# Low-rank products ahead of the grouped heads, and their chain spread over earlier steps

## The reference

```python
p_rwkv, p_pool, p_att, p_gate = jnp.split(hn @ w_in, split_at, axis=-1)
p_rwkv = p + mu_prev * (p_prev - p) + mu_next * (p_next - p)      # token shift
r, k, v, wd, ad, gd = jnp.split(p_rwkv, offs, axis=-1)
w_raw = w0 + einsum('bsel,elc->bsec', tanh(wd), w2)               # two directions e
decay = exp(-exp(-softplus(-w_raw) - 0.5))
a = sigmoid(a0 + einsum('bsel,elc->bsec', ad, a2))
kk = k * k_k / max(norm(k * k_k), 1e-12)                          # per head
k_dir = k * (1 + (a - 1) * k_a)
# a recurrence over 256 tokens, both directions, with r, decay, k_dir, v, kk, a
y_b = pool_w @ (windowed means of p_pool (2, 4, 8, 16 tokens) - p_pool)
y_c = softmax(q @ k.T) @ v                                        # 8 heads, 2 key heads
x = x + (sum over branches of gate * (branch @ w_branch)) @ w_out
x = x + expert_choice_ffn(rms_norm(x))                            # 16 experts
```

## Time and profile before

| | |
|---|---|
| Median of 3 runs | 1749.14 us (1746.7 to 1750.22) |
| Profiled execution | 1747.45 us |
| Its span | 1745.7 us |
| TensorE, VectorE, ScalarE busy | 1559.4, 841.5, 376.7 us |
| Mean DMA rate | 221 GB/s |

### The profile page before, as it was taken

One profiled execution on the slowest core, in us unless ns is written; L12 is line 12 of the kernel. 1 busy time (PEld: TensorE's weight loads), 2 busy tenths in 40 slices (PEclk: granted clock), 3 DMA queues, 4 the chain that ended last, 5 costly groups with the idle time before them and its releaser, 6 DMA issues.

```text
span 1745.7 us, 26458 instructions
## 1 busy us (share of the span) xinstructions
PE 1559.4 (89%) x10938; PEld 1089.6 (62%) x10938; DVE 841.5 (48%) x1699; ACT 376.7 (22%) x952; POOL 2.1 (0%) x6
## 2 busy tenths in 40 slices
PE   9999999999999999999999999999999656656665
PEld 6877878884488786888647878999853112112111
DVE  6676567665577765665646577564531000000001
ACT  4362131110225422311102571111211000000001
POOL 0000000000000000000000000000000000000000
PEclk9999999999999999999999999999999968878868
DMA  9324335344542242453543322121888999999997
GB/s 392 130 74 163 127 119 212 148 190 169 201 173 97 84 183 72 186 192 145 193 175 145 118 99 92 57 75 52 356 366 345 427 425 423 425 424 425 425 420 327
DMA packets 49474, 386.37 MB, mean 221 GB/s; under 512 B 5584, under 2 KB 6096, under 8 KB 9808
## 3 DMA queue, kind: packets, MB, share of 16 engines
q1 hardware_dynamic: 47376, 375.15, 54.0%
q10 hardware_dynamic: 1984, 9.57, 1.4%
HBM read 383.65 MB, written 1.05 MB: 220 GB/s over the span
## 4 chain that ended last, share of the span: by engine, by line
PE 72%; DMA 21%; DVE 3%; ACT 2%; issue 1%; SPq 0%; DVEq 0%; ACTq 0%
PE ps L217 52%; DMA arena<-in_stream 19%; PE ps L2357 3%; PE ps L1096 2%; DMA const<-in_stream 2%; PE ps L1585 2%; PE ps L221 1%; PE ps L1195 1%; PE ps L745 1%; PE ps L1228 1%; PE ps L1254 1%; PE ps L1686 0%; PE ps L2618 0%; PE ps L646 0%; PE ps L2561 0%
## 5 line engine op out<-in xcount | busy, mean ns | idle before, releaser
L217 PE MATMUL ps<-arena 128*128 128x256 f32 (+4 forms) x2364 | 528.9, 484 | 90.7 <-DMA arena<-in_stream 80.8
L217 PEld LDWEIGHTS ps<-arena 128*128 128x128 f32 (+1 forms) x2364 | 308.5, 172 | 266.9 <-DMA arena<-in_stream 128.4
L217 PE MATMUL ps<-ring,arena 128*128 128x256 f32 (+5 forms) x1172 | 323.3, 508 | 37.1 <-DMA ring<-in_stream 31.4
L217 PEld LDWEIGHTS ps<-ring,arena 128*128 128x128 f32 (+1 forms) x1172 | 178.3, 175 | 158.9 <-issue 78.4
L217 PE MATMUL ps<-arena,ring 128*128 128x256 f32 (+1 forms) x1140 | 233.9, 352 | 0.0
L217 PEld LDWEIGHTS ps<-arena,ring 128*128 128x128 f32 x1140 | 190.0, 190 | 28.5 <-issue 9.6
L3038 DVE TENSOR_TENSOR arena<-arena,ps 128x512 f32<-128x512 f32 x8 | 5.5, 687 | 307.6 <-PE ps L2816 307.6
L2816 PE MATMUL ps<-arena 128*32 128x512 f32 x218 | 137.6, 758 | 0.0
L1143 ACT ACTIVATE arena<-arena,small 128x256 f32<-128x256 f32 x112 | 55.7, 498 | 67.0 <-DVE small L1130 50.6
L217 PE MATMUL ps<-arena,spare 128*128 128x128 f32 x510 | 65.5, 278 | 0.0
L217 PEld LDWEIGHTS ps<-arena,spare 128*128 128x128 f32 x510 | 60.4, 192 | 0.7
(11 more groups left out here) (476 smaller groups left out, 2014.1 us busy)
## 6 DMA issues: line engine op xcount, KB each, us to landing
ring<-in_stream SPq DMA_DIRECT2D x131, 1024.0 KB, 4.9
arena<-in_stream SPq DMA_DIRECT2D x112, 1024.0 KB, 17.7
arena<-in_stream SPq DMA_DIRECT2D x24, 2048.0 KB, 37.2
ring<-in_stream SPq DMA_DIRECT2D x12, 2048.0 KB, 32.5
spare<-in_stream SPq DMA_DIRECT2D x6, 2048.0 KB, 37.1
par<-in_stream SPq DMA_DIRECT2D x8, 1024.0 KB, 39.2
const<-in_stream SPq DMA_DIRECT2D x8, 1024.0 KB, 38.8
par<-in_layer_par ACTq DMA_DIRECT2D x3, 1664.0 KB, 8.2
```

The costliest lines, as they stand in the source:

```text
L217: ins = self.pe.e.matmul(out, lhsT, rhs, start=start, stop=stop)
```

## The change

- Units: pooling chunks 15 to 17 move ahead of r and v in `SHIFT_ORDER`, chunk 11 is last. Unit 3 goes into step 0, and all later ones move to steps 1, 3, 4, 5, 6, 7.
- All four low-rank products, and the sigmoids behind them, go between the turn of queries and keys and the first scores. Tanh and the sigmoid that they need go behind unit 1's shift.
- ScalarE: scaled and squared keys go from behind step 2 to behind step 1, key gains from 4 to 2, decay exponentials from beside step 6 to behind step 3, norms from beside step 5 to behind it.
- VectorE: `decay_sums` 2 to 1, `sums_before` 3 to 2, `keys_by_direction` 5 to 3, `clamp_norms` 3 to 4, part of `decayed_keys` 7 to 4, the rest to 5; part of `decayed_queries` 8 to 7. The four windows go from behind the heads into steps 5 to 8, the last subtraction into step 9.

The amount of arithmetic stays the same.

```diff
@@ -97,8 +97,8 @@
-SHIFT_ORDER = (12, 13, 14, 4, 5, 6, 7, 0, 1, 2, 3, 8, 9, 10, 11, 15, 16, 17, 18)
-SHIFT_BESIDE = {0: 4, 1: 5, 3: 6, 4: 7, 6: 8, 7: 9}
+SHIFT_ORDER = (12, 13, 14, 4, 5, 6, 7, 15, 16, 17, 0, 18, 1, 2, 3, 8, 9, 10, 11)
+SHIFT_BESIDE = {0: 3, 1: 4, 3: 5, 4: 6, 5: 7, 6: 8, 7: 9}
...
@@ -2519,6 +2519,11 @@
+def near_chunks(j):
+    return [c for c in SHIFT_ORDER[2 * j:2 * j + 2] if c < 15]
 def second_pe(p, pe, w):
...
@@ -2563,10 +2568,7 @@
-    p.mark["qk"] = p.dve_tiles.opened
-    shifted_unit(3)
-    pe.e.wait_ge(p.act_tiles.drained, p.act_tiles.opened)
-    pe.e.wait_ge(p.dve_tiles.drained, p.mark["qk"])
+    p.mark["qk"], p.mark["qk_act"] = p.dve_tiles.opened, p.act_tiles.opened
...
@@ -2584,18 +2586,18 @@
+    for e in range(2):
+        low_rank("w2", 12, e)
+    for e in range(2):
+        low_rank("a2", 13, e)
+    pe.e.wait_ge(p.act_tiles.drained, p.mark["qk_act"])
+    pe.e.wait_ge(p.dve_tiles.drained, p.mark["qk"])
     def beside_head(t):
-        if t == 1:
-            low_rank("w2", 12, 0)
-        if t == 3:
-            low_rank("a2", 13, 0)
         if t in SHIFT_BESIDE:
...
-        if t == 1:
-            low_rank("w2", 12, 1)
-        if t == 3:
+        if t == 4:
...
-            low_rank("a2", 13, 1)
         if t == 8:
...
@@ -3076,20 +3078,22 @@
-        chunks = [c for c in SHIFT_ORDER[2 * j:2 * j + 2] if c < 15]
+        chunks = near_chunks(j)
+        if not chunks:
+            return
         for o, c in enumerate(chunks):
...
-    for j in range(3):
+    for j in range(2):
...
-    rows_to_columns_evac(p, act, p.qk2, None, 5, True)
-    shift_base(3)
...
+    shift_base(2)
+    rows_to_columns_evac(p, act, p.qk2, None, 5, True)
...
@@ -3106,32 +3110,18 @@
+    for e in range(2):
+        low_rank_gains("w0", p.sig, e)
+    for e in range(2):
+        low_rank_gains("a0", p.iclr, e)
     def beside_head(t):
-        if t == 1:
-            low_rank_gains("w0", p.sig, 0)
-        if t == 3:
-            low_rank_gains("a0", p.iclr, 0)
-        if t in (0, 1, 3, 4):
+        if t in SHIFT_BESIDE:
...
-        if t == 1:
-            low_rank_gains("w0", p.sig, 1)
-        if t == 3:
-            low_rank_gains("a0", p.iclr, 1)
-        if t == 5:
-            act.e.wait_ge(p.sem("norms_in"), 1)
-            act.e.activation(flat(p.kd), flat(p.kd), ACT.Ln).then_inc(act.step(), 1)
-            act.e.wait_ge(act.steps, act.n)
-            act.e.activation(flat(p.kd), flat(p.kd), ACT.Exp, scale=-0.5).then_inc(act.event("norms_out"), 1)
-        if t == 6:
-            act.e.wait_ge(p.sem("sums_ready"), 1)
-            act.e.activation(flat(p.inv_dec), flat(p.dec), ACT.Exp, scale=DECAY).then_inc(act.event("decays_ready"), 1)
-            act.e.wait_ge(p.sem("decays_ready"), 1)
-            act.e.activation(flat(p.dec), flat(p.dec), ACT.Exp, scale=-DECAY).then_inc(act.event("decays_ready"), 1)
-            act.e.activation(flat(p.sig), flat(p.sig), ACT.Exp, scale=-DECAY).then_inc(act.event("decays_ready"), 1)
         if t in (8, 9):
...
     def after_head(t):
-        if t == 2:
+        if t == 1:
...
@@ -3141,7 +3131,7 @@
-        if t == 4:
+        if t == 2:
...
@@ -3151,6 +3141,17 @@
+        if t == 3:
+            act.e.wait_ge(p.sem("sums_ready"), 1)
+            act.e.activation(flat(p.inv_dec), flat(p.dec), ACT.Exp, scale=DECAY).then_inc(act.event("decays_ready"), 1)
+            act.e.wait_ge(p.sem("decays_ready"), 1)
+            act.e.activation(flat(p.dec), flat(p.dec), ACT.Exp, scale=-DECAY).then_inc(act.event("decays_ready"), 1)
+            act.e.activation(flat(p.sig), flat(p.sig), ACT.Exp, scale=-DECAY).then_inc(act.event("decays_ready"), 1)
+        if t == 5:
+            act.e.wait_ge(p.sem("norms_in"), 1)
+            act.e.activation(flat(p.kd), flat(p.kd), ACT.Ln).then_inc(act.step(), 1)
+            act.e.wait_ge(act.steps, act.n)
+            act.e.activation(flat(p.kd), flat(p.kd), ACT.Exp, scale=-0.5).then_inc(act.event("norms_out"), 1)
...
@@ -3307,7 +3308,7 @@
-            dve.e.wait_ge(p.sem("shift_based"), j + 1)
+            dve.e.wait_ge(p.sem("shift_based"), sum(bool(near_chunks(i)) for i in range(j + 1)))
...
@@ -3364,23 +3365,28 @@
-    def decayed_keys():
-        dve.e.wait_ge(dve.steps, dve.n)
+    def decayed_rates():
+        dve.e.wait_ge(p.sem("key_gains"), 1)
...
+    def decayed_keys():
...
+    def passed_queries():
+        dve.e.wait_ge(dve.steps, dve.n)
+        dve.e.wait_ge(p.sem("decays_ready"), 3)
+        for e in range(2):
+            e_.tensor_tensor(p.sig[:, e], p.sig[:, e], p.kk, ALU.mult).then_inc(dve.step(), 1)
     def decayed_queries():
-        dve.e.wait_ge(p.sem("decays_ready"), 3)
...
-        for e in range(2):
-            e_.tensor_tensor(p.sig[:, e], p.sig[:, e], p.kk, ALU.mult).then_inc(dve.step(), 1)
...
@@ -3399,45 +3405,54 @@
-    def windows():
-        z, src, dst = p.zp[0][:, :, 8:8 + S], p.zp[0], p.zp[1]
-        for n in range(4):
-            w = 1 << n
-            lo = 8 - w
-            e_.tensor_tensor(dst[:, n:4, 0:272 - w], src[:, n:4, 0:272 - w], src[:, n:4, w:272], ALU.add).then_inc(dve.step(), 1)
-            if n == 0:
-                e_.tensor_copy(p.pooled, z).then_inc(dve.step(), 1)
-            dve.e.wait_ge(dve.steps, dve.n)
-            e_.tensor_tensor(p.zp_mean[:, n, :], dst[:, n, lo:lo + S], p.c("pool_cnt", 4, S)[:, n, :], ALU.mult).then_inc(dve.step(), 1)
-            dve.e.wait_ge(dve.steps, dve.n)
-            src, dst = dst, src
+    def window(n):
+        w = 1 << n
+        lo = 8 - w
+        src, dst = p.zp[n % 2], p.zp[1 - n % 2]
+        dve.e.wait_ge(dve.steps, dve.n)
+        dve.e.wait_ge(p.dve_tiles.drained, p.mark["shift5"])
+        e_.tensor_tensor(dst[:, n:4, 0:272 - w], src[:, n:4, 0:272 - w], src[:, n:4, w:272], ALU.add).then_inc(dve.step(), 1)
+        if n == 0:
+            e_.tensor_copy(p.pooled, src[:, :, 8:8 + S]).then_inc(dve.step(), 1)
+        dve.e.wait_ge(dve.steps, dve.n)
+        e_.tensor_tensor(p.zp_mean[:, n, :], dst[:, n, lo:lo + S], p.c("pool_cnt", 4, S)[:, n, :], ALU.mult).then_inc(dve.step(), 1)
+    def pooled():
+        dve.e.wait_ge(dve.steps, dve.n)
...
-    shift_rest(3)
     def beside_head(t):
-        if t == 3:
-            sums_before()
         if t in SHIFT_BESIDE:
...
+        if t == 1:
+            decay_sums()
         if t == 2:
-            decay_sums()
+            sums_before()
         if t == 3:
+            keys_by_direction()
+        if t == 4:
...
+            decayed_rates()
         if t == 5:
-            keys_by_direction()
+            decayed_keys()
+            window(0)
         if t == 6:
...
+            window(1)
         if t == 7:
-            decayed_keys()
+            passed_queries()
+            window(2)
         if t == 8:
...
+            window(3)
         if t == 9:
...
+            pooled()
...
-    windows()
...
```

## The result

The changed kernel takes 1751.71 us (median of 19 runs) against 1750.24 us for the kernel before in the same comparison. The ratio is 1.0016, 95% interval 1.001 to 1.0022: slower by 2.8 us (1.8 to 3.9), within the 0.2% that the text called no change, though the interval reaches just beyond it. The ratio is worked out from all of the runs; the two medians lie only 1.5 us apart. The forecast was +3.4 us, as 1752.5. The ratios of the experiments leave out two slow runs, one of e1 (7150.37 us) and one of the kernel before (2107.6 us).

The account below looks back on a forecast made before the run. TensorE was taken to set the time in the heads, with 6.1 us idle. A gate product 1.7 us later plus 1.7 us from the lower clock gave +3.4 us on 1749.14: 1752.5 us, range 1748 to 1756.

Parts of the forecast that it names:

- Which waits the change removes: TensorE in the heads: waits of 1.51, 1.50 and 1.75 us on ScalarE's copies vanish; the 0.74 wait stays.
- The table loads: ScalarE: four of ten function table switches go, 5.1 us, worth only what stands in TensorE's waits.
- The low-rank waits: TensorE at the low-rank products: 0.6 us for the turned query tile, 0.3 us for gains at the third banks.
- The chain that sets item 7's copy: Longest waits from unit 4 through VectorE and ScalarE work put item 7's score copy, with its signal, at 1040.4.
- the round trips: VectorE's token shifts wait for ScalarE's base, behind exponentials that need VectorE's maximum: 1.3 us each time.
- The wait at step 8: TensorE ahead of the gate product idles 5.2 us for VectorE's score bank copy; gate product 1.7 us later.
- The clock: After the 5.2 us wait at step 8 TensorE drops to its lower clock, mostly costing 1.7 us.
- The passage to the end: The experts' weight stream starts on VectorE's signal ending the recurrence, so earlier shifts reach the end one for one.
- The sum: Whole kernel: 1.7 us from the later gate product plus 1.7 from the lower clock, +3.4 us.
- the base of 1749.14: Median time of the kernel before that the forecast started from; its profiled execution took 1747.45 us.
- the clock that stays up: Rival, 15%: gate product after the step 8 wait runs at 2.4 GHz; +1.7 us, 1750.8.
- VectorE keeps up: Rival, 10%: hand-offs overlap more, item 7's copy comes before TensorE asks at step 8; 1744 to 1746 us.

Follow-up runs that it names:

- e1: Changed kernel with the four pooling windows and the last subtraction back behind the heads; 1746.83 us, ratio 0.9985 to the kernel before.
- e5: Changed kernel with the chain back in its old steps and the windows behind the heads, low-rank products still first; 1745.92 us, ratio 0.9983 to before.
- e6: Changed kernel with windows behind the heads, scans ahead of unit 4's copies, normed keys behind item 7's copy; 1743.62 us, ratio 0.9975 to before.
- e2: Changed kernel with VectorE's eight scans of step 1 put ahead of unit 4's copies; 1749.84 us, ratio 1.0006 to the kernel before.
- e4: Changed kernel with normed keys and window 1 moved from step 6 to 7, behind item 7's score copy; 1744.75 us, ratio 0.9969 to before.
- e3: Changed kernel with five unused 128x512 products on TensorE ahead of the wait at step 8; 1751.29 us, ratio 1.0007 to the kernel before.

## Why the prediction was right

- **Which waits the change removes.** Right: all three ScalarE waits went. Only two go with the low-rank part: in e5, which has it alone, one of 1.78 us stays at step 7, so the third is removed by the chain that moved. The text called the waits all that the edit could give back; e5 and e6 also have 1.0 and 1.2 us less busy time of TensorE. The table loads: four fewer; no run takes them away alone, so what they are worth is not shown.
- **The low-rank waits.** 0.6 and 0.3 laid out, 0.48 and 3 x 0.16 = 0.48 measured.
- **The chain that sets item 7's copy.** Its signal was laid out at 1040.4, with the scans at 992.6, item 6's maximum done at 1030.9 and the round trips at 1.3; measured 1039.90, 992.64, 1030.5 and 1.23 for units 7 and 8 (1.90 for unit 6, where the layout added up ScalarE's own steps). The working has a slip: its terms from 1013.6 add up to 1020.7, not 1020.9. e2 (a gain at the chain's head comes out at its end), e1 and e4 (what stands ahead of the copy counts, what stands behind it does not) show its two ends; the links between rest on the trace of the changed kernel alone.
- **The wait at step 8.** 5.2 us laid out, 4.76 measured; the gate product was to be 1.7 us later and was 1.1. This is the term that was over-sized, by half a microsecond: about 0.2 is the slip above, the rest the sum of small hand-offs.
- **The clock.** 1.7 us by the stream's rows; the unit takes 8.43 against 6.74 in e3: 1.7. That it is just the stream's usual loss was in part luck, since single waits there cost between 0.9 and 3.4. The Trainium skill, page "TensorE: Matmul & The Clock Gate", section "Why this matters for your kernels", advises against idle gaps between bursts of products; the trace agrees, in the heads too.
- **The passage to the end.** Whole, by the table's column. The profiled execution is 4.2 us above that of before, 3.0 from the stream's start and 1.2 from what the stream varies by.
- **The sum.** +3.4 forecast, 2.9 at the recurrence's start, 2.8 (1.8 to 3.9) by the runs. As a time, 1752.5 lies 0.8 us from the measured 1751.71, and that is partly luck: the base of 1749.14, a median of three runs, was 1.1 us below the later median of 19, and the forecast step was larger than the measured one.
- **Of the rivals,** the clock that stays up is what e3 makes: it happens only when the wait is filled. VectorE keeps up is what e4 and e6 make, and e1 in part. That rival had 3 to 5 us less than before; by the ratios it is 5.4 (3.5 to 7.4) in e4, 4.4 (2.4 to 6.3) in e6 and 2.6 (1.1 to 4.2) in e1. The chance of 42% for slower by over 0.2% was high for a sum that lay just below that line.
- **Not asked by the prediction:** how good either half is. It treated the change as one; e5 and e1 show that it holds a gain of 3.5 us and a loss of 6.5, of which 5.0 hang on the place of two windows.

## What to carry to other kernels

Before work is moved into an engine's idle time, ask what that engine must hand over next and put the work behind it: here 5.0 us of VectorE's work cost 4.9 us at the gate product, and 1.7 more by the clock, when it stood ahead of one score copy, and 0.3 us when it stood behind (e4). Idle shares don't show this, since VectorE had 28 of 90 us free; laying out each engine's new order with durations of the old trace, hand-off by hand-off, did, to half a microsecond over 73 (966.9 to 1039.9). Several short waits that are gathered into one long one cost more than the wait itself once TensorE's clock falls behind it: here 4.76 us of idle and then 1.7 of slow products.

## What the runs showed of the hardware

Behind 3.06, 4.26 and 4.76 us of idle the loss at the gate unit was the same 1.7 us (8.43 against 6.64 to 6.74 us for 30 records), though the stream's waits had cost between 0.9 and 3.4. Float32 products of 128x512 that nobody reads kept the clock at its higher level when five of them left 0.49 us of the wait, and did not when two left 3.06. In e3 they made the unit behind the wait 1.7 us shorter and the gate product 0.03 us later, counted from the heads' start. That the whole kernel gains by it is seen in one trace and is too small for the runs to show. In the stream a group was slow behind 0.69 us of idle as well, so this short list holds for a dense stage.
